# Linear attention's queries and keys: weight tiles first, with the low-rank product and the gate rounds between tiles 1 and 4

## What is computed

```
proj = h @ w_in
q = heads(proj[..., :nk], dk) * dk ** -0.5          # nk = 4 heads * 128
k = heads(proj[..., nk:2 * nk], dk)
gz = proj[..., 2 * nk + 2 * nv:] @ w_gate_up + b_gate    # 16 columns of proj, then 16 x 512
log_a = heads(jax.nn.log_sigmoid(gz) / GLA_GATE_TEMP, dk)
cum = jnp.cumsum(log_a)                               # inside the recurrence
```

## Time and profile before

| what | value |
|---|---|
| time, median of 3 runs | 1820.53 us |
| lowest and highest run | 1820.46 and 1823.21 us |
| the profiled execution's own time | 1823.0 us |
| its span, first to last instruction | 1821.2 us |
| mean granted TensorE clock | 0.915 |

### The profile page before, as it was taken

The page is one execution under the profiler, slowest core; times in us unless marked ns, Lnnn a source line. Parts: engine busy times, 40 slices in busy tenths (PEclk is TensorE's granted clock), DMA queues, the critical chain, the costliest instruction groups (busy, mean ns, idle before and its releaser), DMA issues. The chain is left out here.

```text
span 1821.2 us, 34391 instructions
## 1 busy us (share of the span) xinstructions
PE 1556.1 (85%) x13422; PEld 1250.5 (69%) x13422; DVE 762.5 (42%) x1144; ACT 621.8 (34%) x1253; POOL 653.6 (36%) x509
## 2 busy tenths in 40 slices
PE   5299983999779499999999579989694999999994
PEld 4278873677557288888788458866473888887883
DVE  0372543777344634444322530017646344442223
ACT  3252331677332333333222322233423333332211
POOL 1103440566202345555433313330233455554331
PEclk9599995999898799999999879997787999999997
DMA  8822324001542123333332102324211233333301
GB/s 248 253 72 61 91 67 139 2 2 48 171 154 59 34 70 93 98 97 105 96 96 74 39 14 82 93 81 134 75 59 35 70 93 96 99 106 96 96 21 49
DMA packets 218551, 158.06 MB, mean 87 GB/s; under 512 B 15687, under 2 KB 203624, under 8 KB 218112
## 3 DMA queue, kind: packets, MB, share of 16 engines
q1 hardware_dynamic: 218444, 156.58, 29.0%
HBM read 145.87 MB, written 19.02 MB: 91 GB/s over the span
## 5 line engine op out<-in xcount | busy, mean ns | idle before, releaser
L288 POOL TENSOR_TENSOR wlo<-wst,whi 128x1024 bf16<-128x1024 f32 (+1 forms) x180 | 424.8, 2366 | 620.3 <-ACT whi L277 620.2
L304 PE MATMUL ps<-hhi,whi 128*128 128x272 f16 x1792 | 504.6, 282 | 34.3 <-PEq L192 34.3
L305 PE MATMUL ps<-hlo,whi 128*128 128x272 bf16 x1792 | 504.6, 282 | 0.0
L306 PE MATMUL ps<-hhi,wlo 128*128 128x272 f16 x1792 | 504.3, 281 | 0.0
L277 ACT CAST whi<-wst 128x1024 f16<-128x1024 f32 (+1 forms) x180 | 196.4, 1104 | 233.0 <-PE ps L306 223.0
L304 PEld LDWEIGHTS ps<-hhi,whi 128*128 128x128 f16 x1792 | 176.9, 99 | 69.8 <-issue 36.0
L306 PEld LDWEIGHTS ps<-hhi,wlo 128*128 128x128 bf16 x1792 | 177.0, 99 | 34.1
L305 PEld LDWEIGHTS ps<-hlo,whi 128*128 128x128 f16 x1792 | 176.8, 99 | 33.8
L304 PE MATMUL ps<-g_hi,whi 128*128 128x272 f16 x704 | 197.0, 280 | 0.0
L305 PE MATMUL ps<-g_lo,whi 128*128 128x272 bf16 x704 | 197.0, 280 | 0.0
L306 PE MATMUL ps<-g_hi,wlo 128*128 128x272 f16 x704 | 196.9, 280 | 0.0
(11 more groups left out here) (341 smaller groups left out, 2364.9 us busy)
## 6 DMA issues: line engine op xcount, KB each, us to landing
wst<-in_ffn_w_up SPq DMA_DIRECT2D x88, 512.0 KB, 3.8
wst<-in_ffn_w_down SPq DMA_DIRECT2D x32, 704.0 KB, 4.7
wst<-in_gla_w_in SPq DMA_DIRECT2D x24, 512.0 KB, 3.7
wst<-in_nsa_w_in SPq DMA_DIRECT2D x20, 512.0 KB, 3.7
chunks<-in_cache_nsa_kv SPq DMA_DIRECT2D x32, 256.0 KB, 3.9
out_win_s<-in_state_win_kv SPq DMA_DIRECT2D x8, 1016.0 KB, 15.0
wst<-in_nsa_w_o SPq DMA_DIRECT2D x8, 512.0 KB, 4.2
qkv<-in_cache_nsa_kv SPq DMA_DIRECT2D x16, 256.0 KB, 3.5
```

Source lines behind the costliest of these rows:

```text
L288: pool.tensor_tensor(core.wlo[:, k, 0:w], core.wst[:, k, 0:w], core.whi[:, k, 0:w], ALU.subtract).then_inc(core.w_lo, 1)
L304: pe.matmul(out, a_hi, b_hi, start=start and j == 0, stop=False)
L305: pe.matmul(out, a_hi, b_lo, start=False, stop=False)
L306: last = pe.matmul(out, a_lo, b_hi, start=False, stop=stop and j == n - 1)
```

## The change

TensorE now begins the stage with weight tiles 0 and 1. Behind tile 1 come the norm-gain product and the low-rank product; behind tile 2 gate rounds 0 and 1; behind tile 3 gate rounds 2 and 3; then tiles 4 to 7. Gate rounds alternate between banks 4 and 5 and banks 6 and 7, and a round waits for the emptying of the round two before it. ScalarE's list follows: the two low-rank copies stand ahead of the copy of tile 2, two gate activations each ahead of the copies of tiles 3 and 4, and Exp and Ln ahead of the copy of tile 6. VectorE's, GpSimd's and SyncE's lists keep their order.

```diff
             @block.tensor
             def _(pe):
-                pe.wait_ge(small_in, 64)
-
-                pe.matmul(ps[:, 6, 0:DV], core.ones[0:1, :], ngrow[:, :], start=True, stop=True).then_inc(low, 1)
-                pe.wait_ge(cast, 2)
...
-                pe.wait_ge(low_taken, 2)
-                for t in range(GH):
-                    pe.wait_ge(z_taken, since(t))
+                def low_rank():
+                    pe.wait_ge(small_in, 64)
+                    pe.matmul(ps[:, 6, 0:DV], core.ones[0:1, :], ngrow[:, :], start=True, stop=True).then_inc(low, 1)
+                    pe.wait_ge(cast, 2)
                     for h in range(2):
-                        last = pe.matmul(ps[:, 4 + h, 0:HALF], up[:, t * DK:(t + 1) * DK],
...
+                    last.then_inc(low, 1)
+
+                def gates(t):
+
+                    pe.wait_ge(low_taken, 2)
+                    pe.wait_ge(z_taken, since(t - 1))
+                    for h in range(2):
+                        last = pe.matmul(ps[:, 4 + t % 2 * 2 + h, 0:HALF], up[:, t * DK:(t + 1) * DK],
                                          lowT[:, h * HALF:(h + 1) * HALF], start=True, stop=True)
                     last.then_inc(z_ready, 1)
...
                         last.then_inc(core.w_used, 1)
+                        if n == 1:
+                            low_rank()
+                        if n in (2, 3):
+                            gates(2 * n - 4)
+                            gates(2 * n - 3)
...
             @block.scalar
                 def body(i):
                     for k in range(4):
+                        if 4 * i + k == 2:
+                            low_rank()
+                        if 4 * i + k in (3, 4):
+                            gates(2 * (4 * i + k) - 6)
+                            gates(2 * (4 * i + k) - 5)
+                        if 4 * i + k == 6:
+                            softplus()
                         act.wait_ge(core.w_used, first + 4 * i + k + 1)
```

More of the change, by code:

```diff
@@ L1967, in _ @@
             def _(pe):
-                pe.wait_ge(small_in, 64)
-                pe.matmul(ps[:, 6, 0:DV], core.ones[0:1, :], ngrow[:, :], start=True, stop=True).then_inc(low, 1)
-                pe.wait_ge(cast, 2)
[L1972 to L1977, removed]
-                pe.wait_ge(low_taken, 2)
-                for t in range(GH):
-                    pe.wait_ge(z_taken, since(t))
-                    for h in range(2):
-                        last = pe.matmul(ps[:, 4 + h, 0:HALF], up[:, t * DK:(t + 1) * DK],
+                def low_rank():
+                    pe.wait_ge(small_in, 64)
+                    pe.matmul(ps[:, 6, 0:DV], core.ones[0:1, :], ngrow[:, :], start=True, stop=True).then_inc(low, 1)
+                    pe.wait_ge(cast, 2)
+                    for h in range(2):
+                        cols = slice(h * HALF, (h + 1) * HALF)
+                        last = product(pe, ps[0:16, 4 + h, 0:HALF], [(a, a) for a in range(KD)],
+                                       lambda a: (gwhi[:, a, :], gwlo[:, a, :]),
+                                       lambda a: (core.hhi[:, a, cols], core.hlo[:, a, cols]), True, True)
+                    last.then_inc(low, 1)
[4 more added lines that the diff above has]
+                        last = pe.matmul(ps[:, 4 + t % 2 * 2 + h, 0:HALF], up[:, t * DK:(t + 1) * DK],
                                          lowT[:, h * HALF:(h + 1) * HALF], start=True, stop=True)
@@ L2004, in _, with low_rank, gates, softplus @@
                 act.copy(gwhi[:, :, :], gw[:, :, :]).then_inc(cast, 1)
[L2005 to L2009, removed]
-                    act.wait_ge(z_ready, t + 1)
[L2011 to L2016, removed]
+                def low_rank():
+                    act.wait_ge(low, 1)
+                    act.copy(gla.ng[:, :], ps[:, 6, 0:DV]).then_inc(low_taken, 1)
+                    act.wait_ge(low, 2)
+                    act.copy(lowT[:, :].rearrange("p (h c) -> p h c", h=2), ps[0:16, 4:6, 0:HALF]
+                             ).then_inc(low_taken, 1)
+                def gates(t):
+                    act.wait_ge(z_ready, t + 1)
+                    act.activation(z[:, t, :].rearrange("p (h c) -> p h c", h=2),
+                                   ps[:, 4 + t % 2 * 2:6 + t % 2 * 2, 0:HALF], ACT.Identity, bias=bias[:, t:t + 1]
+                                   ).then_inc(z_taken, 1)
+                def softplus():
+                    act.wait_ge(steps, 1)
+                    act.activation(gla.cum[:, :, :], gla.cum[:, :, :], ACT.Exp).then_inc(steps, 1)
+                    act.wait_ge(steps, 2)
+                    act.activation(gla.cum[:, :, :], gla.cum[:, :, :], ACT.Ln, bias=1.0).then_inc(steps, 1)
                 def body(i):
                     for k in range(4):
+                        if 4 * i + k == 2:
[5 more added lines that the diff above has]
+                            softplus()
                         act.wait_ge(core.w_used, first + 4 * i + k + 1)
```

## The result

The changed kernel takes 1812.03 us (median of 5 runs, 1809.86 to 1813.78), against 1820.79 for the kernel before on the same chip: a ratio of 0.9946, interval 0.9931 to 0.996. That is 8.8 us less, where 9.8 was forecast, and the time lies inside the range. The profiled execution took 1813.09 us, its span 1811.3.

What follows compares the result with a forecast made beforehand. TensorE, busy 85% of the span, was taken as the bound. Its work ends 12.7 us earlier, the next stage starts 11.5 earlier after VectorE's tail, less 1.7 for half clock: 9.8 us off the median 1820.53, 1810.7; range 1807.0 to 1815.5.

Steps and rivals of the forecast that it cites:

- When TensorE can start: Stage opening: tile 0 needs only the stage to open, so begins 14.64 us after the normalization's last TensorE product, at 1053.55.
- TensorE's own work: Tile 0 to tile 7: tiles, cold start, norm-row and low-rank products, gates sum to 56.7 us; copy 7 starts 12.7 us earlier.
- VectorE's tail: Stage's end: Exp, Ln, VectorE's step and four scans end 1.8 us behind copy 7's start, so VectorE closes the stage.
- The way out: Opening of the next stage: 11.5 us earlier, gap about 2.9 us, half clock behind it costing 1.7, gain 9.8 us.
- no cost at the end: Rival at the stage's end: shorter tail or full clock; 1809.0 without the clock's fall, 1807.8 if 12.7 us come through; chance 0.24.
- The rival of the gates' clock: Gate rounds pull the clock down, 3.7 us a pair: one pair 1814.4 (chance 0.11), both 1818.1 (0.06).

## Why the prediction was right, and where it was not

- *When TensorE can start*: 14.64 us behind the normalization, as forecast from the two feed-forward stages.
- *TensorE's own work*: from tile 0 to copy 7 it took 57.15 us (1054.70 to 1111.85); the sum said 56.9. The parts are: half clock for 3.6 us, so 1.8 (forecast 2.0); norm-gain and low-rank product 6.28 (1067.73 to 1074.01; 6.2); a gate round 1.0 (1.0). That tile 0 was slow for want of work ahead of it, and for no other cause, is shown by the kernel with 61 extra products.
- *VectorE's tail*: the sums end 1.74 us behind the start of copy 7 (forecast 1.8). Moving Exp and Ln by a tile either way moved the stage's end by what the chain says. With no subtraction of GpSimd beside them the four sums take 1268 to 1292 ns each, and the decay's first step, which began while a subtraction ran until 1091.30 (the two rows below), took 3.30 us instead of 2.43, where it costs nothing. That agrees with the Trainium skill (SBUF — State Buffer, "Who interferes with whom"), by which a VectorE instruction with two SBUF inputs contends with a GpSimd instruction that reads SBUF, under an exclusive lock.

```profile
1089.17 2.13 POOL L288 TENSOR_TENSOR wlo<-wst,whi 128x1024 bf16<-128x1024 f32 x1 [5.56 <-ACT whi L277]
1090.29 3.30 DVE L2054 SCALAR_TENSOR_TENSOR gla_cum<-z 128x2176 f32<-128x2176 f32 x1 [31.79 <-ACT z L2022]
```

- *The way out*: the gap is 2.90 us (about 2.9). **The step that was mis-sized** is the clock behind it: I took 1.7 us, and in the changed kernel's profile it was nothing, so the 11.3 us by which the stretch shrank (11.5 forecast) came through whole, where the sum left 9.8. Behind the same gap it cost 1.7 in the kernel with one pair of banks. It happens in some executions and not in others, and so does the very row that I took the 1.7 from the earlier trace rows: behind that early opening, at 134 to 137 us in all eleven profiles and with a gap of 2.42 to 2.52 us, TensorE ran at half clock in five and at full clock in six, as in the two views below, from the kernel with Exp and Ln a tile earlier. What decides between them these runs don't show. I had given "no cost at the end" 0.24 against 0.50 for the forecast; these rows speak for about even chances. That the profiled time came within 0.2 us of the 1813.2 of the sum is therefore partly luck, 1.5 us too little here against 1.15 lost ahead of the stage.

```profile
136.59 0.27 PE L304 MATMUL ps<-whi,hhi 128*128 128x256 f16 x1 [2.52 <-PEq L192]
```

```profile
136.90:140.30 3.40, 3.40 (x34) 3.04 (x33) 2.19 (x1) 0.00 (x0) 0.00 (x0) 1.00 0.02 5
```

- *The rival of the gates' clock* did not come, but it stood nearer than the text says. I argued from the waits that were gone. The experiments show two things that keep the clock up: rounds without waits (the second pair of banks) and, by one profile, not four in a row (the pairs a tile apart). The loss that I gave it, 3.7 us a pair, is more than the kernel with one pair of banks shows: 7.9 us for both, of which 2.5 are waits, so 2.7 a pair.

## What to carry to other kernels

Work with few rows and with waits between its products should stand in small pieces between dense tiles, with enough banks that no piece waits; here one pair of banks less cost 7.9 of the 11.3 us. After moving a chain behind the tiles, count it from the last thing that it waits for to the barrier: the engine that was idle now ends the stage. And where a stage opens cold, look at how long TensorE idles ahead of it; products that nobody uses, up to 1.5 us before the opening, gave about 2 us for each of three stages.

## What was not expected of the hardware

Whether a gap at the opening of a stage brought the clock down is not told by its length alone. Gaps of 2.57 and 2.58 us behind the extra products did in all four places, gaps of 2.42 to 2.52 us at the early opening in five profiles of eleven, gaps of 2.90 to 2.92 us at the end of this stage in one of three. Gaps of 1.50 to 1.85 us at openings with weight tiles, with the clock up ahead of them, did in none of ten. Chance could have spared one opening with 61 products, but all three, and the seven others of these ten, speak for the shorter gap. This holds between dense products only: in the sparse attention of the kernel before, the clock stood at 0.54 right behind a gap of 1.94 us (333.4 to 336.8).

And behind 4.14 us of gate products without a pause among them, with a wait of 0.69 us ahead, the clock fell in the one profile that has them so, though TensorE was busy throughout.
